# Attention of a hybrid encoder: maxima and exponentials of a block's scores over two halves of 1024 keys in place of four pieces of 512

## What is computed

```python
def one(qblk):                      # 128 queries of each head
    s = jnp.einsum('bqhd,bkhd->bhqk', qblk, k, preferred_element_type=jnp.float32) * scale
    p = jax.nn.softmax(s, axis=-1).astype(v.dtype)
    return jnp.einsum('bhqk,bkhd->bqhd', p, v)
```

## Time and profile before

| | us |
|---|---|
| median of 3 runs | 2371.25 (2369.34 to 2372.03) |
| the profiled execution | 2368.78 |
| its span, first to last instruction | 2366.7 |
| mean granted TensorE clock | 0.989 of full speed |
| TensorE matmul busy | 2257.7 (95% of the span) |
| VectorE busy | 1406.8 (59%) |
| ScalarE busy | 1139.5 (48%) |
| GpSimd busy | 1028.1 (43%) |

### The profile page before, as it was taken

One profiled execution on the slowest core, in us unless ns is written; L12 is line 12 of the kernel. 1 busy time (PEld: TensorE's weight loads), 2 busy tenths in 40 slices (PEclk: granted clock), 3 DMA queues, 4 the chain that ended last, 5 costly groups with the idle time before them and its releaser, 6 DMA issues. The chain is left out here.

```text
span 2366.7 us, 34587 instructions
## 1 busy us (share of the span) xinstructions
PE 2257.7 (95%) x11426; PEld 1895.1 (80%) x11426; DVE 1406.8 (59%) x2145; ACT 1139.5 (48%) x2147; POOL 1028.1 (43%) x763
## 2 busy tenths in 40 slices
PE   4999998999998999999999989998999999999998
PEld 3788887888887778777777868887888888877886
DVE  6333335434344777777777751215899999984342
ACT  3544434222223655555555545556555566653332
POOL 5422222222222433333232242322998999982454
PEclk8999999999999999999999999999999999999999
DMA  8334423343434534343333233331111211253653
GB/s 297 134 136 147 142 94 134 123 149 120 151 126 132 156 96 116 92 111 92 108 97 103 61 132 127 121 133 36 45 50 49 67 58 40 76 177 108 178 159 108
DMA packets 196117, 271.15 MB, mean 115 GB/s; under 512 B 10532, under 2 KB 137764, under 8 KB 191398
## 3 DMA queue, kind: packets, MB, share of 16 engines
q1 hardware_dynamic: 191398, 261.43, 34.6%
q10 hardware_dynamic: 4608, 8.39, 0.9%
HBM read 183.27 MB, written 86.51 MB: 114 GB/s over the span
## 5 line engine op out<-in xcount | busy, mean ns | idle before, releaser
L2338 POOL TENSOR_TENSOR conv_g<-conv_g,product 128x1024 f32<-128x1024 f32 x160 | 384.8, 2407 | 34.3 <-ACT product L2387 24.6
L2485 DVE SCALAR_TENSOR_TENSOR ps_b<-u,cols,ps_b 128x1024 f32<-128x1024 f32 x304 | 391.6, 1288 | 9.2
L2601 PE MATMUL ps_a<-ho_hi,wp_lo 128*128 128x512 f32 x768 | 300.6, 391 | 6.8 <-DVE h_left L2541 6.8
L2602 PE MATMUL ps_a<-h_left,wp_hi 128*128 128x512 f32 x768 | 299.8, 390 | 0.0
L2603 PE MATMUL ps_a<-ho_hi,wp_hi 128*128 128x512 f32 x768 | 299.6, 390 | 0.0
L2387 ACT ACTIVATE product<-u,cols 128x1024 f32<-128x1024 f32 x160 | 183.3, 1151 | 169.7 <-POOL conv_g L2338 168.4
L1590 ACT ACTIVATE pt_hi<-ps_pt 128x512 fp32r<-128x512 f32 x256 | 154.5, 604 | 198.9 <-PE ps_pt L1786 198.7
L1701 DVE TENSOR_TENSOR pt_lo<-ps_pt,pt_hi 128x512 fp32r<-128x512 f32 x256 | 175.6, 686 | 119.7 <-ACT pt_hi L1590 114.9
L1645 POOL TENSOR_TENSOR v_lo<-v_st,v_hi 128x512 fp32r<-128x512 f32 x64 | 84.2, 1316 | 236.9 <-DVE v_hi L1677 236.9
L1691 DVE TENSOR_REDUCE mx<-ps_s 128x1 f32<-128x512 f32 x248 | 166.9, 682 | 23.2 <-PE ps_s L1778 22.2
L2601 PEld LDWEIGHTS ps_a<-ho_hi,wp_lo 128*128 128x128 f32 x768 | 144.8, 189 | 38.6 <-DVE h_left L2541 8.7
(11 more groups left out here) (445 smaller groups left out, 5619.0 us busy)
## 6 DMA issues: line engine op xcount, KB each, us to landing
scratch_ret_pack<-pack SPq DMA_DIRECT2D x14, 1280.0 KB, 5.5
pack<-scratch_ret_pack SPq DMA_DIRECT2D x14, 1280.0 KB, 6.6
k_st<-scratch_k_t SPq DMA_DIRECT2D x64, 256.0 KB, 3.5
v_st<-scratch_v SPq DMA_DIRECT2D x64, 256.0 KB, 3.7
ada<-in_ada_w_dram SPq DMA_DIRECT2D x16, 768.0 KB, 6.4
wp_raw<-in_od_w_in_dram SPq DMA_DIRECT2D x24, 512.0 KB, 3.9
xt<-in_x_dram SPq DMA_DIRECT2D x16, 512.0 KB, 6.1
ada<-in_ada_w_dram SPq DMA_DIRECT2D x8, 1024.0 KB, 7.8
```

Source lines behind the costliest of these rows:

```text
L2338: pool.tensor_tensor(half(conv_g, h), half(conv_g, h), product[adds(c, i, h) % 2][:], ALU.add).then_inc(added, 1)
L2485: dve.scalar_tensor_tensor(acc[h], units(c, k, h), params(c, k), acc[h], ALU.mult, ALU.add).then_inc(tap, 1)
L2601: pe.matmul(dst, lo[:, k, :], h_hi[:, k, t], start=k == 0, stop=False)
L2602: pe.matmul(dst, hi[:, k, :], h_lo[:, k, t], start=False, stop=False)
```

## The change

The maxima and the exponentials of a block go over two halves of two banks (1024 keys) each. The PSUM tensors are allocated as pairs of banks, in the same order as before. `mx` and `sums` have two columns per block. An exponential adds 2 to `exp_done`, so the waits on it keep their numbers; VectorE's maximum i waits for both banks of its half (`s_done` at 2i + 2 of the block). TensorE's order and matmuls are the same, and so is ScalarE's order with two exponentials: first half, left-over `turn_hi`, second half, then the rest. On VectorE the maximum of the first half stands where that of bank 1 stood, behind `turn_lo` of step 0 and, in block 1, the sums; that of the second half stands where that of bank 3 stood.

```diff
-        mx = sb("mx", [P, QB])
+        mx = sb("mx", [P, 2])
...
-        sums = [sb(f"sums{i}", [P, QB, QB]) for i in range(2)]
+        sums = [sb(f"sums{i}", [P, QB, 2]) for i in range(2)]
...
-        ps_s = [bank(f"ps_s{i}") for i in range(4)]
-        ps_pt = [bank(f"ps_pt{i}") for i in range(2)]
-        ps_o = [bank(f"ps_ot{i}") for i in range(2)]
+        def two_banks(name):
+            return ctx.enter_context(nc.psum_tensor(name, [P, 2 * BANK], F32))
+
+        def each(two):
+            return [two[:, i * BANK:(i + 1) * BANK] for i in range(2)]
+
+        two_s = [two_banks(f"ps_s{i}") for i in range(2)]
+        two_pt, two_o = two_banks("ps_pt"), two_banks("ps_ot")
+        ps_s = each(two_s[0]) + each(two_s[1])
+        ps_pt, ps_o = each(two_pt), each(two_o)
...
+        def half_of(n, b, i):
+
+            return [two_pt, two_o][i][:] if first(n) and b % 2 else two_s[i][:]
...
-            def exps(n, s, b, kb):
-
-                if kb == 0:
+            def exps(n, s, b, i):
+
+                if i == 0:
                     act.wait_ge(bias_ready, 4 * n + b + 1)
...
-                act.activation(probs[s][b][:, kb * BANK:(kb + 1) * BANK], bank_of(n, b, kb), ACT.Exp, bias=bias[b % 2][:],
-                               scale=SCALE, accum_out=sums[s][:, b, kb:kb + 1]).then_inc(exp_done, 1)
+                act.activation(probs[s][b][:, 2 * i * BANK:2 * (i + 1) * BANK], half_of(n, b, i), ACT.Exp, bias=bias[b % 2][:],
+                               scale=SCALE, accum_out=sums[s][:, b, i:i + 1]).then_inc(exp_done, 2)
...
-                    for i in range(4):
+                    for i in range(2):
                         if b > 0 and score:
                             exps(n, s, b - 1, i)
...
-            def block_max(n, b, kb):
-                hold(dve, st, s_done, 16 * n + 4 * b + kb + 1)
-                dve.tensor_reduce(mx[:, kb:kb + 1], bank_of(n, b, kb), AX.X, ALU.max).then_inc(max_done, 1)
+            def block_max(n, b, i):
+                hold(dve, st, s_done, 16 * n + 4 * b + 2 * i + 2)
+                dve.tensor_reduce(mx[:, i:i + 1], half_of(n, b, i), AX.X, ALU.max).then_inc(max_done, 1)
 
             def block_bias(n, b):
-                hold(dve, st, max_done, 16 * n + 4 * b + 4)
+                hold(dve, st, max_done, 8 * n + 2 * b + 2)
...
                     for i in range(4):
-                        if score:
-                            block_max(n, b, i)
+                        if score and i % 2:
+                            block_max(n, b, i // 2)
```

More of the change, by code:

```diff
@@ L1400, in attention @@
         ada = sb("ada2", [P, 3 * D // 2])
-        mx = sb("mx", [P, QB])
+        mx = sb("mx", [P, 2])
         m1 = sb("m1", [P, 1])
         bias = [sb(f"bias{i}", [P, 1]) for i in range(2)]
-        sums = [sb(f"sums{i}", [P, QB, QB]) for i in range(2)]
+        sums = [sb(f"sums{i}", [P, QB, 2]) for i in range(2)]
         total = sb("total", [P, QB])
         inv = [sb(f"inv{i}", [P, QB]) for i in range(2)]
-        def bank(name):
-            return ctx.enter_context(nc.psum_tensor(name, [P, BANK], F32))
-        ps_s = [bank(f"ps_s{i}") for i in range(4)]
-        ps_pt = [bank(f"ps_pt{i}") for i in range(2)]
-        ps_o = [bank(f"ps_ot{i}") for i in range(2)]
+        def two_banks(name):
[6 more added lines that the diff above has]
+        ps_pt, ps_o = each(two_pt), each(two_o)
         v_in = [sem(f"v_in{i}") for i in range(QB)]
@@ L1498, in bank_of @@
         def bank_of(n, b, kb):
-            return (ps_pt + ps_o)[kb][:] if first(n) and b % 2 else ps_s[kb][:]
+            return (ps_pt + ps_o)[kb] if first(n) and b % 2 else ps_s[kb]
+        def half_of(n, b, i):
+            return [two_pt, two_o][i][:] if first(n) and b % 2 else two_s[i][:]
         def last(n, k):
@@ L1589, in turn_hi @@
                     act.wait_ge(pv_done, 16 * m + kt - 3)
-                act.activation(pt_hi[kt % 4][:], ps_pt[kt % 2][:], ACT.Copy).then_inc(pthi_done, 1)
+                act.activation(pt_hi[kt % 4][:], ps_pt[kt % 2], ACT.Copy).then_inc(pthi_done, 1)
             def w_piece(n, b, i):
@@ L1620, in group @@
                             act.wait_ge(o_turned, n - 2)
-                        act.activation(o_t[:], ps_o[s][:], ACT.Copy).then_inc(o_out, 1)
+                        act.activation(o_t[:], ps_o[s], ACT.Copy).then_inc(o_out, 1)
                     if score and not last(n, 1):
@@ L1700, in turn_lo @@
                 hold(dve, st, pthi_done, 16 * m + kt + 1)
-                dve.tensor_tensor(pt_lo[kt % 4][:], ps_pt[kt % 2][:], pt_hi[kt % 4][:].bitcast(F32),
+                dve.tensor_tensor(pt_lo[kt % 4][:], ps_pt[kt % 2], pt_hi[kt % 4][:].bitcast(F32),
                                   ALU.subtract).then_inc(ptlo_done, 1)
@@ L1794, in values_of @@
                     pe.wait_ge(out_ready, m - 1)
-                pe.matmul(ps_o[sl][:], v_lo[:, kt, :], pt_hi[kt % 4][:], start=kt == 0, stop=False)
-                pe.matmul(ps_o[sl][:], v_hi[:, kt, :], pt_lo[kt % 4][:], start=False, stop=False)
-                pe.matmul(ps_o[sl][:], v_hi[:, kt, :], pt_hi[kt % 4][:], start=False, stop=kt == NK - 1).then_inc(pv_done, 1)
+                pe.matmul(ps_o[sl], v_lo[:, kt, :], pt_hi[kt % 4][:], start=kt == 0, stop=False)
+                pe.matmul(ps_o[sl], v_hi[:, kt, :], pt_lo[kt % 4][:], start=False, stop=False)
+                pe.matmul(ps_o[sl], v_hi[:, kt, :], pt_hi[kt % 4][:], start=False, stop=kt == NK - 1).then_inc(pv_done, 1)
             def group(n, s, score, values, write):
```

## The result

| | before | after |
|---|---|---|
| median, us | 2371.25 (5 runs, 2368.65 to 2372.07) | 2383.35 (5 runs, 2380.92 to 2384.43) |
| ratio after / before | | 1.0051, 95% interval 1.0037 to 1.0065 |
| profiled execution, us | 2368.78 | 2384.43 |
| attention, first score matmul to last output transpose | 625.57 | 637.14 |
| the rest of the profiled span | 1741.1 | 1745.6 |

What follows compares the result with a forecast made beforehand. The prediction took TensorE's queue plus its gaps as the bound. Later bank releases summed 6.0 + 5.3 + 3.7 + 1.5 - 0.3 = 16.2 us onto the 2371.25 us median, giving 2387.4 us; eight-in-ten range 2381 to 2394, own range 2384 to 2392.

Steps and rivals of the forecast that it cites:

- longer first Exp: ScalarE's first exponential, now over 1024 columns instead of 512, ends and frees its banks 0.43 us later.
- into block 1, each: First scores into block 1, groups 2 to 15: TensorE already waits, so the full 0.43 us counts, 14 times.
- into block 3, each: First scores into block 3, groups 1 to 15: 0.43 us less 0.08 to spare, 15 times, 5.3 us.
- into block 0, usual, each: First scores into block 0 at the ten places not behind a loop jump: 0.37 us each, 3.7 us.
- into block 2, each: First scores into block 2: TensorE's stop for the left-over turn_lo absorbs the 0.35 us delay, so 0.
- start: First scores to the output transposes in group 2's time: 2.65 us more, 1.5 of it from group 1.
- 13 intervals: The 13 stretches between output transposes of successive groups, up to group 15: 13.5 us more in sum.
- tail: Last two stretches of the attention: 0.35 us more, less 0.3 for group 16's last exponentials, put at 0.
- Rival (a): The bias becomes the gate: later second maximum makes the exponential start late too; up to 7 us, 2394 us, chance 0.12.
- Rival (b): Faster: shorter ScalarE and VectorE busy times shrink TensorE's stops in block 2, up to 4 us, 2367 us; chance 0.03.
- Four follow a jump of the loop: Four places into block 0 where TensorE stops about 0.93 us for late VectorE; stop absorbs the delay, so 0.
- VectorE's shorter queue around the jump: Downward allowance in the forecast's own range: fewer VectorE operations near the loop jump may give back 1 or 2 us.

Runs made afterwards that it cites:

- after_relaxed: Changed kernel, but each exponential into block 1 waits only for the transposes that read the probs columns it overwrites; 2372.64 us, ratio 0.9999 to before.
- exp_one_three: Changed kernel with the first exponential over one bank and the second over three; 2378.27 us, ratio 1.0023 to before.
- max_halves_both: max_halves with the finer wait on transposes into block 1 and VectorE's left-over turn_lo ahead of the next queries' operations; 2346.99 us, ratio 0.9887 to before.
- max_halves: Changed kernel with the exponentials back to four single banks, maxima still over two halves; 2365.26 us, ratio 0.9969 to before.
- max_halves_padded: max_halves with a one-column memset and the removed maximum's wait put back into VectorE's queue, two per block; 2373.22 us, ratio 0.9999 to before.
- exp_one_one_two: Changed kernel with the exponentials in three operations of one, one and two banks; 2365.32 us, ratio 0.9972 to before.
- exp_halves: Changed kernel with the maxima back to four single banks, exponentials still over two halves; 2384.21 us, ratio 1.0052 to before.
- exp_three_one: Changed kernel with the first exponential over three banks and the second over one; 2402.10 us, ratio 1.0127 to before.
- after_low_first: Changed kernel with VectorE's left-over turn_lo of block 1 ahead of the three operations on the next queries; 2374.25 us, ratio 1.0004 to before.
- after_padded: Changed kernel with a one-column memset on VectorE in place of each removed maximum, with that maximum's wait; 2383.79 us, ratio 1.0043 to before.

## Why the prediction came out as it did

**What held.** The direction, the mechanism and most of the terms.

| term | forecast, us | measured |
|---|---|---|
| longer first Exp | 0.43 | 0.42 |
| into block 1, each | 0.43 | 0.39 to 0.43 |
| into block 3, each | 0.35 | 0.33 to 0.38, with block 2 |
| into block 0, usual, each | 0.37 | 0.21 to 0.33 |
| into block 2, each | 0 | 0 |
| start | 2.65 (1.5 + 0.43 + 0.35 + 0.37) | 2.68 |
| 13 intervals | 13.5 | 9.16 |
| tail | 0 (0.35 - 0.3) | -0.27 |
| sum | 16.2 | 11.6 |

A place's number is how much longer it takes from the first score load of the block before to its own. The scores of block 2 come 0.33 to 0.38 late, the stop of block 2 takes that up, and those of block 3 are late by as much again.

That a stop into block 1 counts is shown by `after_relaxed`: with the early release its waits are 10.3 us shorter and the 13 intervals 9.4. That the cost goes by the size of the first piece is shown by the row of 1, 2 and 3 banks, and that the second piece counts too once it is three banks long by `exp_one_three`. That block 2 absorbs is shown by equal 4.06 us on both sides and by `max_halves_both`. Rival (a) is refuted for this order: within the loop the exponential starts at least 0.34 us behind the bias. Rival (b), a gain from shorter busy times, fell with `max_halves` and `max_halves_padded`, which have the shorter maxima and a usual interval of 38.37 and 38.38 against 38.36 before, and with `exp_one_one_two`, where a piece fewer is worth nothing. (The Trainium skill's page "VectorE: DVE Perf Modes", section "The TRN2 errata — SBUF-src ops pay a fixed extra latency per instruction", says of operations that read SBUF that a single large tile pays the latency once and many small ones pay it each. Those here read PSUM, and the trace shows the like in their busy time: four Exps take 2.80 us a block and two 2.24, four maxima 2.73 and two 2.44. The time of the kernel does not hang on it.) The one gain that there is came from another side.

**What failed.** The step "Four follow a jump of the loop, where VectorE comes back late ... The stop ends at a time of its own ... So 0 for these". I took the stop as given. It was absorbed as I said only where it lasts: `exp_halves` has 39.98 us on average in the groups with a jump against 39.31 before, 0.67 more, where a usual group has 0.98 more; 0.3 was absorbed. But the change takes the stop itself away. Its four excesses over a usual group (39.58 + 39.45 + 38.98 + 39.24 - 4 x 38.36) are 3.8 us. With it gone, a group with a jump costs the change 0.05 us and not 0.78: 2.9 us of the 4.3 that are missing in the 13 intervals. The rest is the terms of blocks 3 and 0, mis-sized: 1.0 a usual group against the forecast 1.15, 9 x 0.15 = 1.4 us. The spare time there was as I had read it: at blocks 0 the read-out ended 0.05 to 0.14 us ahead of the load, 0.05 of which is the release. And the load does come later by what I had said, 0.34 at blocks 3 and 0.34 to 0.45 at blocks 0. But a wait of the load is not a loss of the same size. The load behind it, which had followed after 0.23 us, follows a waiting load after 0.11, as in the rows into a block 3 above, and 0.12 us of each new wait comes back. That is 0.24 us a group, against which the wait into block 1, which was there already, grew by 0.48 to 0.52 and not by 0.43. In `exp_three_one` no wait is new, and its group is longer by the full 3 x 0.42. I had allowed 1 or 2 us for "VectorE's shorter queue around the jump", as a size, without asking why VectorE came late there: the row said so, its bracket named `turn_hi` as the releaser of a wait of 2.96 us, but ScalarE had ended it at 1052.63, 2.9 us before. Both misses lie on one side: 2383.35 is inside the range of 2381 to 2394, and just under the 2384 to 2392 that the forecast had for itself.

**The clock in group 1.** The start fits the forecast in sum (2.68 against 2.65), but the parts don't add up: `max_halves` is 0.55 and `exp_halves` 0.08 under the kernel before. Into block 1 of group 1 they do: 0.55 and 0.46 alone, 1.11 together, forecast 1.0, bias and exponential in series. Behind it TensorE's granted clock, the share behind the busy times here, differs from kernel to kernel; from 790 to 810 us of the kernel after, of `after_low_first` and of `after_padded`:

```profile
790.00:810.00 20.00, 16.28 (x76) 12.72 (x75) 13.95 (x22) 11.07 (x20) 8.98 (x8) 0.91 0.42 121
```

```profile
790.00:810.00 20.00, 16.28 (x85) 13.02 (x84) 13.88 (x24) 10.28 (x19) 9.46 (x7) 1.00 0.39 111
```

```profile
790.00:810.00 20.00, 16.28 (x71) 12.62 (x70) 12.99 (x25) 10.49 (x20) 8.48 (x7) 0.83 0.42 118
```

| kernel | time at half clock in group 1, us | from block 1's first score load to block 2's, us |
|---|---|---|
| before | 3.41 | 9.31 |
| `max_halves`, `exp_halves` | 0 | 8.28, 8.23 |
| after | 3.41 | 10.37 |
| `after_low_first`, `after_relaxed` | 0 | 8.78, 8.78 |
| `after_padded` | 6.83 | 11.52 |
| `exp_one_three` | 3.41 | 9.83 |

Just ahead of it TensorE had stood for the first exponential: 2.39 us before, 3.42 after, 2.93 in `max_halves` and 2.88 in `exp_halves`. That is why the start of `max_halves` is shorter: 0.55 more into block 1, and 1.03 less behind it. The change lost 1.6 us to the clock (10.37 against 8.78), and the kernel before 1.0 or more; up to 0.6 us of the 2.68 may be the clock's, which the forecast did not have, and that the start came out within 0.03 us is in part luck.

**What stays open.** Why the clock fell in some of these kernels and not in others: the length of TensorE's stand alone doesn't tell, since it fell behind 2.39 us and not behind 2.88 or 2.93.

## What to carry to other kernels

When an operation that empties PSUM banks is made larger, ask what the first bank's next writer has to spare, and size the first piece by that; the later pieces may be merged as far as their banks are needed later (1, 1, 2 was as fast as 1, 1, 1, 1). Fewer instructions on an engine with idle time are worth nothing by their duration, but in a loop their number can be: look at each engine's first instructions behind the jump and at the instruction queues' packets. A stop of a bottleneck engine that ends at a time of its own absorbs delays ahead of it, so removing both is worth more than the two alone suggest.

## What I had not expected of the hardware

Behind each jump of the loop VectorE stood 2.5 to 4.1 us for nothing that the profile names, in the four kernels that have four VectorE operations for a block's maxima and not two (before, `exp_halves` and the two padded ones), with 59 packets on the instruction queue 14 each time; in all kernels with 16 fewer in a round of the loop (8 blocks x 2) the pauses are not there, and the queue has 37 to 39. Here a memset of 0.06 us and its wait do as much as a maximum of 0.68. That queue 14 brings VectorE's instructions is inferred: packets and pauses go together, and VectorE starts 2.0 to 2.1 us after the start of the packet that falls into its pause, 16 times of 16. The profile doesn't name the queue's engine, and at which number of instructions the pause sets in was not tried.

The load behind a weight load of TensorE that has waited follows after 0.11 us and not after 0.23, so in these kernels a new wait of the load costs 0.12 us less than its length.

An Exp from PSUM takes 0.70, 1.12 and 1.54 us for 512, 1024 and 1536 columns, with a read-out of 0.2 us behind each that the release waits for: 0.42 us per 512 columns and 0.28 besides.
